# A projection and its two mixers written as one block: tiles in another order, query norms folded into the scores, tanh in place of sigmoid and silu

## What is computed

```python
proj = a @ w_in                        # 1024 x 3352
forget = lb + (1 - lb) * sigmoid(f);  key = 1 - forget;  query = silu(q) * 128**-0.5
G = cumsum(log(forget))                # in chunks of 64 tokens
o = causal(q*exp(G-Gref) @ (k*exp(Gref-G)).T) @ v + q*exp(G) @ S   # S: state, chunk by chunk
o_hg = rmsnorm(o) * silu(g)
qh = rmsnorm(q_heads) * 64**-0.5       # 8 query heads, 2 kv heads
kc, vc = compress(k), compress(v)      # gelu(windows @ w1) @ w2, 15 of them
o_nsa = g0*softmax(qh kc) vc + g1*softmax(qh ks) vs + g2*softmax(qh kw) vw
h = x + concat(o_hg, rmsnorm(o_nsa)) @ w_out
```

## Time and profile before

| | us |
|---|---|
| median of 3 runs | 2068.8 |
| lowest, highest | 2066.91, 2072.6 |
| the profiled execution | 2070.71 |
| its span | 2068.9 |

### The profile page before, as it was taken

The page is one execution under the profiler, slowest core; times in us unless marked ns, Lnnn a source line. Parts: engine busy times, 40 slices in busy tenths (PEclk is TensorE's granted clock), DMA queues, the critical chain, the costliest instruction groups (busy, mean ns, idle before and its releaser), DMA issues. The chain is left out here.

```text
span 2068.9 us, 33672 instructions
## 1 busy us (share of the span) xinstructions
PE 1998.7 (97%) x13538; PEld 1761.6 (85%) x13538; DVE 1452.3 (70%) x2212; ACT 1058.8 (51%) x1977; POOL 34.5 (2%) x33
## 2 busy tenths in 40 slices
PE   8978999999999999999989999999999999998998
PEld 7868999999999888888877867877778888778998
DVE  7766599988898678888587757577764227667554
ACT  5664444467776555445573256452223217555444
POOL 0000000000000000000010000100000001000000
PEclk9989999999999999999999999999999999999999
DMA  6404556554444677777546420235673333124663
GB/s 240 150 1 130 176 184 186 190 166 135 146 138 145 197 253 262 257 254 251 163 133 206 161 72 17 92 133 186 240 280 108 102 99 101 32 73 154 194 190 126
DMA packets 94827, 326.90 MB, mean 158 GB/s; under 512 B 10321, under 2 KB 15825, under 8 KB 94673
## 3 DMA queue, kind: packets, MB, share of 16 engines
q1 hardware_dynamic: 94672, 324.75, 48.4%
HBM read 323.66 MB, written 1.05 MB: 157 GB/s over the span
## 5 line engine op out<-in xcount | busy, mean ns | idle before, releaser
L330 DVE TENSOR_TENSOR wlo<-raw,whi 128x1024 fp32r<-128x1024 f32 (+1 forms) x502 | 613.3, 1224 | 334.8 <-ACT whi L324 331.6
L324 ACT ACTIVATE whi<-raw 128x1024 fp32r<-128x1024 f32 (+1 forms) x502 | 525.4, 1049 | 378.2 <-PE ps L705 365.6
L703 PE MATMUL ps<-x_hi,whi 128*128 128x512 f32 (+1 forms) x976 | 333.1, 341 | 12.6 <-DVE x_lo L506 8.2
L704 PE MATMUL ps<-x_lo,whi 128*128 128x512 f32 (+1 forms) x976 | 329.1, 337 | 0.0
L705 PE MATMUL ps<-x_hi,wlo 128*128 128x512 f32 (+1 forms) x976 | 328.9, 337 | 0.0
L703 PE MATMUL ps<-xT_hi,whi 128*128 128x256 f32 x1136 | 324.7, 286 | 3.2 <-DVE xT_lo L504 2.9
L704 PE MATMUL ps<-xT_lo,whi 128*128 128x256 f32 x1136 | 318.3, 280 | 0.0
L705 PE MATMUL ps<-xT_hi,wlo 128*128 128x256 f32 x1136 | 316.7, 279 | 0.0
L703 PEld LDWEIGHTS ps<-x_hi,whi 128*128 128x128 f32 x976 | 183.4, 188 | 45.0 <-issue 14.3
L703 PEld LDWEIGHTS ps<-xT_hi,whi 128*128 128x128 f32 x1136 | 214.3, 189 | 3.5 <-issue 3.5
L704 PEld LDWEIGHTS ps<-xT_lo,whi 128*128 128x128 f32 x1136 | 214.5, 189 | 0.0
(11 more groups left out here) (435 smaller groups left out, 3311.5 us busy)
## 6 DMA issues: line engine op xcount, KB each, us to landing
raw<-peer_u_t SPq DMA_DIRECT2D x128, 512.0 KB, 3.5
raw<-peer_v_t SPq DMA_DIRECT2D x128, 512.0 KB, 4.0
raw<-ffn_in_t SPq DMA_DIRECT2D x88, 512.0 KB, 4.4
x<-ada_t SPq DMA_DIRECT2D x64, 512.0 KB, 4.5
raw<-ffn_out_t SPq DMA_DIRECT2D x44, 512.0 KB, 3.7
raw<-qkv_t SPq DMA_DIRECT2D x36, 512.0 KB, 4.1
gated<-ada_t SPq DMA_DIRECT2D x32, 512.0 KB, 5.7
raw<-w_in_t SPq DMA_DIRECT2D x24, 512.0 KB, 3.8
```

Of the source, the lines that this page charges most:

```text
L324: act.activation(whi[:, n % SPLIT, 0:w], raw[:, g % RAW, 0:w], ACT.Copy).then_inc(hi_done, 1)
L330: dve.tensor_tensor(wlo[:, n % SPLIT, 0:w], raw[:, g % RAW, 0:w], whi[:, n % SPLIT, 0:w].bitcast(F32), ALU.subtract).then_inc(lo_done, 1)
L703: pe.matmul(place, wh, xh, start=start, stop=False, skip_group_check=shared)
L704: pe.matmul(place, wh, xl, start=False, stop=False, skip_group_check=shared)
```

## The change

The two blocks become one. The mixers' functions are methods of the classes `OnTensor`, `OnScalar` and `OnVector` now, and `Woven` calls their `at(w)`; behind piece 27 (`w == 28`) each runs its `end`.

- Tile order: keys, f, queries, hq, the 280 columns, g, v (before: keys, queries, f, hq, 280, v, g). The decays so stand at w = 10 to 17, the windows of the compression at 10 to 13.
- Queries are not normed. Their squares are summed by token (16 short matmuls, `q_root`); the reciprocal root `q_rstd` is the factor of the exponents and of the maxima, and the root times the slope (`q_slope`) that of the bias. The queries' gain goes into the keys'. Four reciprocals of 256 columns and four products go.
- Sigmoid of the gates, silu and Gelu are made from tanh: ACT takes the tanh, DVE does the rest. A silu's drain thus is one ACT and one DVE instruction. Twice its value comes out, and the half goes into other factors.
- Scores 0 to 3, bias 0 to 2, exponents 0 to 2, the compressed scores, turn 0 and the transposes of the decays stand between pieces 20 to 27.
- In `end` the HGRN products, states and outputs stand between attention steps 1 to 7.

The diff, cut to this:

```diff
-CMP_AT = [13 + 3 * m for m in range(2 * CMP_LEN * 64 // 1024)]
+CMP_AT = [10 + m for m in range(2 * CMP_LEN * 64 // 1024)]
...
+                if w == 15:
+                    pe.wait_ge(heads_squared, 2)
+                    for qb in range(TB):
+                        for c in range(NSA_G):
+                            at = 2 * (NSA_G * qb + c)
+                            mm = pe.matmul(ps[:, 6, at:at + 2], qsq[:, c, qb * P:qb * P + P], k("ones64", 0, P).rearrange("p (h n) -> p h n", h=2)[:, :, 0],
+                                           start=True, stop=True)
...
+                if w == 20:
+                    pe.wait_ge(values_spread, 1)
+                    pe.wait_ge(act_evacuated.h, act_evacuated.at(4))
+                    self.scores(pe, 0)
+                if w == 21:
+                    self.compare(pe)
+                if w == 22:
+                    self.scores(pe, 1)
+                if w == 24:
+                    self.scores(pe, 2)
+                if w == 25:
+                    self.turn(pe, 0)
+                if w == 26:
+                    self.hg_turn(pe)
+                if w == 27:
+                    self.scores(pe, 3)
+                if w == 28:
+                    self.end(pe)
...
+                self.hg_scores(pe)
+                self.turn(pe, 1)
+                pe.wait_ge(act_evacuated.h, act_evacuated.at(10))
+                pe.wait_ge(dve_evacuated.h, dve_evacuated.at(8))
+                self.attend(pe, 0)
+                self.scores(pe, 4)
+                self.hg_state(pe, 0)
+                self.hg_state(pe, 1)
...
+                                   scale=qrstd[:, qb, c, n // 2:n // 2 + 1], accum_out=sums[:, i % 3, n:n + 1]).then_inc(nsa_exp, 1)
...
+                if w == 18:
+                    act.wait_ge(heads_summed, 2)
+                    act.activation(hn[:, :, :].rearrange("p c t -> p (c t)"), ps[:, 4, :], ACT.Sqrt, bias=eps[:, :], scale=1.0 / 64).then_inc(heads_root, 1)
+                    act.activation(flat(qroot), ps[:, 6, 0:2 * TB * NSA_G], ACT.Sqrt, bias=eps[:, :], scale=1.0 / 64).then_inc(heads_root, 1)
...
+                if w == 21:
+                    act.wait_ge(act_evacuated.h, act_evacuated.at(7))
+                    act.wait_ge(dve_evacuated.h, dve_evacuated.at(5))
+                    act.activation(gates[:, :, :], nv[:, :, 256:280], ACT.Tanh, scale=0.5).then_inc(halved, 1)
+                if w == 22:
+                    self.exps(act, 0)
+                if w == 23:
+                    self.compare(act)
+                if w == 24:
+                    self.exps(act, 1)
+                if w == 25:
+                    self.scale(act, 0)
+                if w == 26:
+                    self.copies(act, 0)
+                if w == 27:
+                    self.exps(act, 2)
+                    self.hg_copies(act)
...
+                    ins = dve.scalar_tensor_tensor(out=sc[:, i % 2, half * w:half * w + w].rearrange("p (a t) -> p a t", a=2),
+                                                   in0=dist[:, qb:qb + 1, 0:SEEN[i]].broadcast_to([P, 2, SEEN[i]]), scalar=qslope[:, qb, c, half:half + 1],
+                                                   in1=ps[:, SCORE_BANK + half, 0:w].rearrange("p (a t) -> p a t", a=2), op0=ALU.mult, op1=ALU.add)
...
+                low = nm[:, i % 2, :].rearrange("p (h a) -> p h a", h=2)
+                dve.tensor_tensor(low, low, qrstd[:, qb, c, :].unsqueeze(2).broadcast_to([P, 2, 2]), ALU.mult).then_inc(nsa_max, 1)
...
+                dve.tensor_tensor(cs[:, :, :, :], ps[:, TURN_BANK:TURN_BANK + 2, 0:TB * NSA_G * N_CMP].rearrange("p h (u n) -> p h u n", n=N_CMP),
+                                  qrstd[:, :, :, :].rearrange("p b c h -> p h (b c)").unsqueeze(3).broadcast_to([P, 2, TB * NSA_G, N_CMP]), ALU.mult).then_inc(cmp_link, 1)
...
+                if w == 14:
                     dve.wait_ge(compressing, len(CMP_AT))
                     dve.tensor_tensor(ch(d4), at_end(G, HG_CHUNK - 1), ch(G), ALU.subtract).then_inc(decays, 1)
...
+                                             op0=ALU.add, op1=ALU.mult).then_inc(hidden_act, 1)
                     dve.wait_ge(exp_parts, 1)
...
+                if w == 17:
                     dve.wait_ge(exp_parts, 3)
                     dve.tensor_tensor(fl(d4), fl(key), fl(d4), ALU.mult)
...
+                    dve.reciprocal(hn[:, 0, :], hn[:, 0, :]).then_inc(heads_rstd, 1)
+                    dve.wait_ge(curved, 3)
+                    dve.tensor_tensor(v("cond", 0, 2 * C), v("cond", 0, 2 * C), tcond[:, :], ALU.mult)
+                    self.key_head(dve, 0)
+                if w == 19:
+                    dve.reciprocal(hn[:, 1, :], hn[:, 1, :]).then_inc(heads_rstd, 1)
+                    dve.wait_ge(heads_root, 2)
+                    dve.reciprocal(flat(qrstd), flat(qroot)).then_inc(heads_rstd, 1)
+                    dve.tensor_tensor(flat(qslope), flat(qroot), mk("slopes"), ALU.mult).then_inc(heads_rstd, 1)
+                    self.key_head(dve, 1)
+                    dve.wait_ge(cmp_root, 1)
+                    dve.reciprocal(crs[:, :], csq[:, :]).then_inc(heads_rstd, 1)
+                    dve.wait_ge(heads_rstd, 5)
+                    dve.scalar_tensor_tensor(out=kcn[:, :], in0=ps[:, 5, 64:64 + N_CMP], scalar=v("nsa_k", 0), in1=crs[:, :], op0=ALU.mult, op1=ALU.mult).then_inc(kcn_done, 1)
+                    dve.tensor_tensor(vblk[:, :, :], ps[:, 5, P:2 * P].unsqueeze(1).broadcast_to([P, NSA_G, P]),
+                                      k("rows").unsqueeze(2).broadcast_to([P, NSA_G, P]), ALU.mult).then_inc(values_spread, 1)
...
+                if w == 21:
+                    self.bias(dve, 0)
+                if w == 22:
...
+                    self.compare_begin(dve)
+                if w == 23:
+                    self.bias(dve, 1)
+                if w == 24:
+                    dve.wait_ge(curved, 4)
+                    self.scale(dve, 0)
+                if w == 26:
+                    self.bias(dve, 2)
+                if w == 27:
+                    self.scale(dve, 1)
                     dve.wait_ge(exp_parts, 4)
...
+            def end(self, dve):
+                self.bias(dve, 3)
+                self.hg_mask(dve)
+                self.scale(dve, 2)
+                self.bias(dve, 4)
+                self.hg_state(dve, 1)
+                self.scale(dve, 3)
+                self.compare_end(dve)
+                self.bias(dve, 5)
+                self.hg_state(dve, 2)
...
+        def twice_silu(n, dst):
+            return ("wide", n * P, slice(0, T), lambda act, place: act.activation(dst, place, ACT.Tanh, scale=0.5),
+                    lambda dve, place: dve.scalar_tensor_tensor(out=dst, in0=dst, scalar=1.0, in1=place, op0=ALU.add, op1=ALU.mult))
...
         product_stage(at_in, aH, [
             (4, 2, 512, [first(0), both(1, pair_of(cin, 0), ACT.Copy), first(2), dve_both(3, pair_of(nqk, 4))]),
+            (4, 2, 512, [first(0), both(1, pair_of(sig, 0), ACT.Sigmoid), first(2), both(3, pair_of(sig, 2), ACT.Sigmoid)]),
             (4, 2, 512, [first(0), both(1, pair_of(nqk, 0), ACT.Copy), first(2), dve_both(3, pair_of(nqk, 2))]),
-            (4, 2, 512, [first(0), both(1, pair_of(sig, 0), ACT.Sigmoid), first(2), both(3, pair_of(sig, 2), ACT.Sigmoid)]),
-            (4, 2, 512, [first(0), both(1, pair_of(qs, 0), ACT.Silu), first(2), both(3, pair_of(qs, 2), ACT.Silu)]),
-            (4, 2, 280, tall_n), (4, 2, 512, tall_v),
-            (4, 2, 512, [first(0), both(1, pair_of(gate, 0), ACT.Silu), first(2), both(3, pair_of(gate, 2), ACT.Silu)])],
+            (4, 2, 512, [first(0), twice_silu(1, pair_of(qs, 0)), first(2), twice_silu(3, pair_of(qs, 2))]),
+            (4, 2, 280, tall_n),
+            (4, 2, 512, [first(0), twice_silu(1, pair_of(gate, 0)), first(2), twice_silu(3, pair_of(gate, 2))]),
+            (4, 2, 512, tall_v)],
             before=Norm(hT, T, lambda c, s: v("mix_norm", c), parts=aH), sync=load_start, packed=True, woven=Woven())```

DVE in the projection, before, from the drain of tile 1 on: the reciprocals of the query norm, one behind each split.

```order
L1271 COPY nqk<-ps 128x512
L1226 RECIPROCAL head_rstd<-head_rstd 128x256
L330 TENSOR_TENSOR wlo<-raw,whi 128x1024
L1226 RECIPROCAL head_rstd<-head_rstd 128x256
L330 TENSOR_TENSOR wlo<-raw,whi 128x1024
L1195 SCALAR_TENSOR_TENSOR nqk<-nqk,vec,head_rstd 128x256 x2
L330 TENSOR_TENSOR wlo<-raw,whi 128x1024 x2
L1226 RECIPROCAL head_rstd<-head_rstd 128x256
```

984 lines of the change are left out of this document (467 added, 517 removed).

## The result

| | before | after |
|---|---|---|
| median, us (20 runs each) | 2068.5 | 2071.8 |
| lowest, highest | 2066.7, 2072.6 | 2069.5, 2076.2 |
| span of the profiled execution | 2068.9 | 2070.5 |
| w_out's first product at | 165.65 | 166.55 |
| next stage's first product at | 199.93 | 202.20 |

The ratio is 1.0015, 95% interval 1.0008 to 1.0022: about 3 us slower, less than the 0.3% named in the prediction. Forecast were 2070.1 and no measurable change. The number is right, and by luck: of the terms that it was summed from, four were off and cancelled. Added up to w_out's first product, the forecast was 113.6 (bias 3) + 34.1 (ring) + 16.3 (tail) + 2.9 (clock) = 166.9 us. Measured were 115.3 + 38.1 + 13.2 = 166.6, with the clock inside the three: +1.7, +4.0, -3.1 and -2.9. At the next stage's first product the changed kernel is 2.3 us behind in these two profiles, and about 3 us in the time.

A forecast was written before the change was run, and what follows sets the result against it. TensorE, busy 97%, bounds the kernel: time comes only from its waits or lower clock. Gain -9.3, ring +7.7 and clock +2.9 give +1.3 on 2068.8, so 2070.1 us; own range 2066 to 2074, with rivals 2061 to 2078.

The forecast's parts named there:

- Floor and stall: Projection: last product at 105.2 us if PE never waits; PE waits for VectorE's splits add 6.7, giving 111.9.
- Half clock at pieces 19 and 20: Projection: PE waits ahead of these pieces bring on a half clock stretch, costing 1.5 us.
- Bias 3 at 113.6: VectorE's bias 3 starts 1.7 us after the last projection product at 111.9; before, it started at 122.95.
- Six table loads at nothing: ScalarE loses six of fourteen table loads, 1.28 us each; they were costed at nothing of their own.
- Ring 34.1: Chain across engines from bias 3 to scale 7: 34.1 us against 26.4 before, giving back 7.7.
- Compared turn's half clock: Mixer: PE's 4.2 us wait for step 3's first copy brings on half clock, costing 1.5 us.
- Tail unchanged, 16.3: From the square roots to w_out's first product, order kept: 16.3 us as before.
- rival A: Tail keeps 2.4 GHz, returning 4.8 us: -6.4 in all, 2062.4 us; chance 0.18.
- Behind w_out nothing may differ: After w_out starts, no difference; more than 1 us would mean something unseen is at work.
- Rival B: Half clock holds through pieces 20 to 27, and likewise at the second place: +7.9, 2076.7 us; chance 0.20.
- Rival C: Bias 1 and 2 delay splits 23 to 27; steps stand between pieces, not under: 5 us more, 2075; chance 0.07.

The follow-up runs named there:

- a1: Against the changed kernel: key norm's reciprocal root made on ScalarE by Ln and Exp, taking two reciprocals off VectorE; 2068.0 us, ratio to before 0.9991.
- a3: Against the changed kernel: ScalarE's copies of step 3 put ahead of the exponents of step 5; 2067.2 us, ratio to before 0.9990.
- b3: Against the changed kernel: first state ahead of scale 2 and exponents 4, HGRN squares ahead of exponents 6 and 7; 2069.2 us, ratio to before 1.0001.
- b2: Against the changed kernel: one-column activations at pieces 4, 8 and 13 add six table loads; 2070.7 us, ratio to before 1.0008.
- a2: Against the changed kernel: the 32 exponents take immediate factor 1.0 instead of the query norm's pointer; 2070.2 us, ratio to before 1.0006.
- b1: Against the changed kernel: query norm left out of the ring (immediate exponent factor and bias slope, no product of maxima); 2067.6 us, ratio to before 0.9992.
- a4: Against the changed kernel: ten unread identity matmuls fill PE's wait ahead of w_out's first product; 2069.6 us, ratio to before 1.0003.
- d2: Against the changed kernel: unread identity matmuls fill all four long PE waits between projection and w_out; 2069.0 us, ratio to before 0.9996.
- b4: Against the changed kernel: work placed between pieces 20 and 27 moved behind piece 27, same order; 2076.8 us, ratio to before 1.0035.

## Why the prediction was right, step by step

The sum was +1.3 us at w_out and +0.9 was measured. By its terms:

- **Floor and stall.** The waits were 2.33, 1.40 and 1.17 us, forecast 2.3, 3.2 and 1.2. The second was short because piece 19 ran at half clock and so ended 1.2 us later, nearer to VectorE's end. (The list of VectorE's work adds up to 11.5 us and not 12.) The last product ended at 112.9, forecast 111.9. Less the waits (4.9) and piece 19's 1.2 that is 106.8, so the floor of 105.2 was 1.6 too low; the projection starting 0.3 later (13.99, 13.70) is a part of it, the rest isn't taken apart. Experiment a1 shows the cause of the stall to be right, and its price.
- **Half clock at pieces 19 and 20, +1.5: wrong, 0.** It lay where PE had to wait for VectorE anyway. Counting wait and half clock both, one behind the other, is the error; one hides the other: from piece 19 to piece 20 it is 4.44 us here and 4.45 at full clock in a3. In other executions of the same instructions it fell at 82 to 86 instead, the second wait was 2.64 and piece 24 came 1.2 us later, so the term is not zero always; and in b3 there was none in the projection. PE in a3, pieces 20 and 24, the half clock of a3, and pieces 20 to 24 of b3:

```profile
80.98 0.35 PE L704 MATMUL ps<-aT_hi,whi 128*128 128x256 f32 x1 [2.64 <-DVE wlo L331]
99.75 0.48 PE L704 MATMUL ps<-whi,aT_hi 128*128 128x512 f32 x1 [1.20 <-DVE wlo L331]
```

```profile
82.00:85.50 3.50, 3.50 (x20) 3.28 (x18) 1.46 (x2) 1.95 (x3) 0.00 (x0) 0.52 0.76 226
81.00:98.00 17.00, 15.83 (x137) 13.71 (x135) 12.99 (x21) 8.51 (x19) 0.00 (x0) 1.00 0.38 124
```

- **Bias 3 at 113.6: 1.7 us too early.** 1.0 from the last product, 0.7 from the last drain of hg_v, which stands behind both w_out splits on VectorE.
- **Six table loads at nothing: right where ScalarE has slack** (b2), with the one wait of 0.8 us counted apart.
- **Ring 34.1: 4.0 us too short**, the largest error. The sum had 1.5 for the half clock at the compared turn in a term of its own; with it the ring is 2.5 short. The exponents were priced by a row of before without the pointer to their factor: 2.0 by the rows, 2.4 by a2. The bias pointer and the product of the maxima together cost the 1.0 that had been reckoned for the product alone (b1: 3.4 in all). The waits for the state (2.66, forecast 2.1) and for the copy (4.74, forecast 4.2) are longer by the same exponents, which stand ahead of both (a2: 2.27 and 4.27), and are not to be added. Both mechanisms were named, and a3 and b3 show that each was one line's place in ScalarE's queue.
- **Compared turn's half clock +1.5: right in kind.** It lasted from 131.8 to 138.8; no run takes its cost apart from the copy's.
- **Tail unchanged, 16.3: wrong, 13.2.** Full clock returned at 155.7 and not at 158.3. This is a part of rival A, for which the prediction asked a whole tail at full clock. Tails in the runs lie between 13.2 and 17.0, with the same instructions.
- **"Behind w_out nothing may differ": wrong for this profile.** The w_out block began with 6.3 us at half clock in place of 3.05, 1.4 us at the next stage. The wait ahead of it is equal (2.48, 2.47), so it could not be read from that row. It belongs to the execution and not to the change: with the same w_out block and the same wait, w_out's first product to the next stage's is 34.3 us in before, 35.7 in after, and between 34.2 (b1) and 35.8 (a1) in the runs without fillers. What decides it in one execution is open. It goes when the wait is filled (a4, d2).
- **Rival A** had the mixer's idle PE at 13.9 us; by the earlier trace rows it is 14.2. **Rival B** did not occur (clock 1.00 from 98.50 to 112.91). **Rival C** is excluded by b4.

The direction follows, in the two profiles: 9.3 us were to be gained at bias 3 and 7.6 were; 7.7 were to be given back in the ring and 11.7 were (38.1 less 26.4); the clock gave 3.1 in the tail and took 1.4 at w_out. Together that is 2.3 us at the next stage.

What stays open: where in an execution the half clock falls. It lies at 77 to 81 in some, at 82 to 86 in others and at neither place in b3, with the same instructions up to there. The Trainium skill (TensorE: Matmul & The Clock Gate, What's actually happening) says that the chip watches PE's activity by a count that runs on by itself and does not start with the kernel, so that the place varies; the two places agree with that, and no run here tests it. The profile of one execution can be 1 to 4 us off by that alone. So a2 and b3 show no gain at w_out while their ratios are 1.9 and 2.9 us lower, the first of which is within its uncertainty of 2.4.
